# Cache pages fetched by GpSimd gathers instead of SyncE transfers, in a hybrid decoder step

## The reference

```python
def step(carry, phys):                      # one page of every sample
    c_blk = cache_ckv[layer, phys]          # (8, 128, 256)
    kp_blk = cache_kpe[layer, phys]         # (8, 128, 32)
    kn_blk, v_blk = _decompress(c_blk, w_ukv, g_kn)   # keys with RMS norm, values
    return _merge(carry, _attn_partial(qn, qp, kn_blk, kp_blk, v_blk, None)), None

carry, _ = lax.scan(step, init, page_table.T)
```

## Time and profile before

| | us |
|---|---|
| median of 3 runs | 1328.28 |
| the runs | 1329.59, 1326.9, 1328.28 |
| span of the profiled execution | 1324.8 |
| total time of the profiled execution | not listed apart from the span |
| TensorE busy in it | 1272.1 |
| VectorE, ScalarE, GpSimd busy | 716.4, 455.3, 152.3 |

### The profile page before, as it was taken

One profiled execution on the slowest core, in us unless ns is written; L12 is line 12 of the kernel. 1 busy time (PEld: TensorE's weight loads), 2 busy tenths in 40 slices (PEclk: granted clock), 3 DMA queues, 4 the chain that ended last, 5 costly groups with the idle time before them and its releaser, 6 DMA issues. The chain is left out here.

```text
span 1324.8 us, 25998 instructions
## 1 busy us (share of the span) xinstructions
PE 1272.1 (96%) x9479; PEld 741.2 (56%) x9479; DVE 716.4 (54%) x1781; ACT 455.3 (34%) x1108; POOL 152.3 (11%) x182
## 2 busy tenths in 40 slices
PE   6999999889999999999999988999999999989898
PEld 4545677656666666665545545666545455445343
DVE  4001448654666666564768776778666666530331
ACT  3001354233343434342445333443444444310220
POOL 0000326400010102033302320000000000000000
PEclk9999999999999999998999989999999999998999
DMA  6421121111111111310331113311343212101001
GB/s 214 161 81 52 34 64 33 52 40 38 37 34 43 38 34 39 72 42 20 95 98 46 41 37 122 126 53 37 101 120 107 84 55 66 39 0 36 16 16 36
DMA packets 82994, 81.48 MB, mean 62 GB/s; under 512 B 18946, under 2 KB 76611, under 8 KB 82868
## 3 DMA queue, kind: packets, MB, share of 16 engines
q1 hardware_dynamic: 80452, 73.87, 18.7%
q10 hardware_dynamic: 2416, 5.96, 1.3%
HBM read 75.72 MB, written 4.07 MB: 60 GB/s over the span
## 5 line engine op out<-in xcount | busy, mean ns | idle before, releaser
L499 PE MATMUL PS<-wk,c_T 128*128 128x512 f32 x1024 | 495.1, 607 | 0.0
L624 DVE TENSOR_REDUCE ssq<-sq__69 128x8 f32<-128x512 f32 x256 | 175.1, 684 | 182.4 <-ACT sq__69 L553 181.2
L499 PEld LDWEIGHTS PS<-wk,c_T 128*128 128x128 f32 x1024 | 176.9, 193 | 152.0 <-issue 139.5
L553 ACT ACTIVATE sq__69<-PS 128x512 f32<-128x512 f32 x256 | 152.6, 596 | 315.3 <-PE PS L499 314.3
L1482 PE MATMUL PS<-xnT,w_ring 128*128 128x276 f32 x416 | 102.6, 404 | 0.0
L1320 PE MATMUL PS<-w_ring,xnT 128*128 128x424 f32 x256 | 95.3, 529 | 0.9 <-DVE xnT L976 0.9
L1482 PEld LDWEIGHTS PS<-xnT,w_ring 128*128 128x128 f32 x416 | 78.9, 193 | 21.1 <-issue 4.1
L455 PE MATMUL PS<-cst,c_ring 128*128 128x128 f32 x512 | 80.0, 279 | 6.4 <-DVE dots_s L619 5.0
L455 PEld LDWEIGHTS PS<-cst,c_ring 128*128 128x128 f32 x512 | 60.6, 144 | 45.0 <-issue 40.5
L1320 PEld LDWEIGHTS PS<-w_ring,xnT 128*128 128x128 f32 x256 | 48.5, 193 | 45.0 <-issue 45.0
L2690 PE MATMUL PS<-w_g,nT 128*128 128x512 f32 x128 | 56.1, 595 | 0.0
(11 more groups left out here) (533 smaller groups left out, 1854.8 us busy)
## 6 DMA issues: line engine op xcount, KB each, us to landing
c_ring<-in_cache_ckv SPq DMA_DIRECT2D x256, 128.0 KB, 2.8
w_ring<-in_w_in SPq DMA_DIRECT2D x4, 1696.0 KB, 12.3
w_ring<-in_w_in SPq DMA_DIRECT2D x9, 512.0 KB, 5.1
r_ring<-in_cache_kpe SPq DMA_DIRECT2D x256, 16.0 KB, 1.7
w_o<-in_w_out SPq DMA_DIRECT2D x8, 512.0 KB, 4.5
w_g<-in_w_ple_gate SPq DMA_DIRECT2D x8, 512.0 KB, 3.6
xn<-in_x_prompt SPq DMA_DIRECT2D x4, 512.0 KB, 10.8
w_ring<-in_w_in SPq DMA_DIRECT2D x2, 1024.0 KB, 5.5
```

What stands on the lines that cost most here:

```text
L499: mm = pe.matmul(PS[:, NORM[v % 2], :], c_T[:, u % 2, k, t * P:(t + 1) * P], wk[:, k], start=(k == 0), stop=(k == 1))
L553: nc.scalar.activation(sq_[:, v % 2, :], PS[:, NORM[v % 2], :], ACT.Square).then_inc(no_sb, 1)
L624: dve.tensor_reduce(ssq[:, u % 2, t * H:(t + 1) * H], sq_[:, v % 2, :].rearrange("p (h c) -> p h c", h=H), AX.X, ALU.add).then_inc(red_sb, 1)
```

## The change

GpSimd requests all pages, as indirect transfers: each takes a column of row numbers, one a partition. VectorE builds two tables of them once (`gather_rows`, near the end of the preparation) from the page table, which is now loaded to all partitions: `token_rows` = page x 128 + partition, and `group_rows` = page x 32 + lane. Four gathers of 128 rows of 1 KB bring a step's latents, so a tile is now one page; one gather of 128 rows of 512 B brings its rotary keys. SyncE issues no pages; where its weight loads were placed by `on_sp.go`, they wait for semaphores of the other work. With the new layout each 32x32 block of the rotary tile can be turned by itself: VectorE does that in one instruction from `r_ring` to r_T, and TensorE's transpose and ScalarE's copy are gone. The `go` calls of GpSimd stand between its own work.

```diff
-        def latent_pages(u, page):
+        def at_step(u):
+            b, j = divmod(u, STEPS)
+            return j * BS + b
+
+        def latent_pages(u):
+            rows_of = io["cache_ckv"].rearrange("n p c -> (n p) c")
             for x in range(GT):
-                p4 = slice(32 * x, 32 * x + 32)
-                nc.sync.dma_start(c_ring[p4, u % RING, :, 0:KVL], ...)
+                at = at_step(u) * GT + x
+                nc.gpsimd.indirect_dma_start(c_ring[:, u % RING, x, 0:KVL], None, rows_of,
+                                             bass.IndirectOffsetOnAxis(ap=token_rows[:, at:at + 1], axis=0)
+                                             ).then_inc(c_in[u % RING], 16)
+
+        def pages_pool():
+            pool = nc.gpsimd
+            rows_of = io["cache_kpe"].rearrange("n (p t) c -> (n p) (t c)", t=GT)
             for u in range(NSTEP):
                 if u >= RING:
+                    pool.wait_ge(vv_ps, u - RING + 1)
+                    pool.sem_inc(slot_taken, 1)
                 if u >= ahead_pages:
+                    latent_pages(u)
                 if u >= R_RING:
-                    sp.wait_ge(tn_ps, u - R_RING + 1)
+                    pool.wait_ge(tn_sb, u - R_RING + 1)
+                nc.gpsimd.indirect_dma_start(r_ring[:, u % R_RING, :], None, rows_of,
+                                             bass.IndirectOffsetOnAxis(ap=group_rows[:, at_step(u):at_step(u) + 1], axis=0)
+                                             ).then_inc(r_in[u % R_RING], 16)
                 yield
...
-            def turn_r(u):                      # TensorE
-                pe.wait_ge(r_in[u % R_RING], 16 * GT * (u // R_RING + 1))
-                pe.wait_ge(k1_sb, u + 1)
-                pe.transpose(PS[:, TURN, 0:P], r_ring[:, u % R_RING, :], ident).then_inc(tn_ps, 1)
...
-            def turned_r(u):                    # ScalarE
-                act.wait_ge(tn_ps, u + 1)
-                nc.scalar.copy(r_T[:], PS[:, TURN, 0:P]).then_inc(tn_sb, 1)
...
+            def turned_r(u):                    # VectorE, at t == 0 ahead of scales(u - 1)
+                dve.wait_ge(r_in[u % R_RING], 16 * (u // R_RING + 1))
+                if u >= 1:
+                    dve.wait_ge(rp_ps, u)
+                dve.transpose(r_T[:].rearrange("c (p s) -> c s p", s=GT),
+                              r_ring[:, u % R_RING, :].rearrange("p (s c) -> p s c", s=GT)).then_inc(tn_sb, 1)
...
+                def gather_rows():              # VectorE, at p == 11 of the preparation
+                    dve.wait_ge(pages_in, 16)
+                    for x in range(GT):
+                        p4 = slice(32 * x, 32 * x + 32)
+                        ins = dve.tensor_scalar(group_rows[p4, :], pages[p4, x::GT], 32.0, con("lane")[p4, :], ALU.mult, ALU.add)
+                    ins.then_inc(group_idx, 1)
+                    dve.wait_ge(group_idx, 1)
+                    dve.tensor_scalar(token_rows[:], pages[:], float(P), con("token"), ALU.mult, ALU.add).then_inc(token_idx, 1)
...
+                    if p == 11:                 # GpSimd, behind diff(11)
+                        pool.wait_ge(token_idx, 1)
+                        pool.wait_ge(rw_ps, sum(c <= len(chunks) - 2 for c in chunk_of))
+                        for u in range(ahead_pages):
+                            latent_pages(u)
+                on_pool.go(PREP_SLOTS)          # behind p == 12
...
             for i in range(NP):                 # chunk_pool
+                on_pool.go(3)
                 pool.wait_ge(lc_sb, i + 1)
                 (three low products)
+                on_pool.go(7)
                 if i >= 1:
                     gated(i - 1)
+                on_pool.go(7)
...
+            on_pool.go(6)                       # seqs_pool
             for j in range(PAIRS):
                 if j == 1:
+                    on_pool.go(4)
                     gated(NT - 2)
                 (wait for gh_ps, six spread products)
+                on_pool.go(2)
+            on_pool.go(2)
             gated(NT - 1)
+            on_pool.go(4)
...
+            on_pool.go(2)                       # lat_pool; go(7) before each wait for h_ref, the rest at its end
...
-                    on_sp.go(2)                 # SyncE, w_o loads; w_g and wukv3 likewise on acc_sb
+                    sp.wait_ge(sc_ps, 2 * k + 1)
```

More of the change, by code:

```diff
@@ L18 @@
 I32 = mybir.dt.int32
+U32 = mybir.dt.uint32
 ALU = mybir.AluOpType
@@ L100, in shape_constants @@
     parts += [("headones", (s // HN == t // HN))]
-    parts += [("ones", np.ones((P, P)))]
+    parts += [("token", s), ("lane", s % 32)]
     parts += [("mod32", (s % 32 == t % 32))]
@@ L220, in build @@
         cols = place("cols", [P, NCOLS])
+        group_rows = place("group_rows", [P, NSTEP], U32)
         nat = place("nat", [P, NT, NAT])
@@ L241, in build @@
         nmax = place("nmax", [P, BS])
-        pages = place("pages", [1, BS * NPG], I32)
+        pages_at_ = place.at
+        pages = place("pages", [P, BS * NPG], I32)
+        token_rows = Region(nc, pages_at_, place.at)("token_rows", [P, BS * NPG], U32)
         sq_at_ = place.at
@@ L412, in build @@
         at_v, at_t = slice(0, KVL + 1), slice(0, P)
-        def page_numbers(u):
+        def at_step(u):
             b, j = divmod(u, STEPS)
-            return [nc.sync.value_load(pages[0:1, (j * BS + b) * GT + x:(j * BS + b) * GT + x + 1], min_val=0,
-                                       max_val=io["cache_ckv"].shape[0] - 1) for x in range(GT)]
-        def latent_pages(u, page):
+            return j * BS + b
+        def latent_pages(u):
+            rows_of = io["cache_ckv"].rearrange("n p c -> (n p) c")
@@ L508, in pages_pe @@
                 ahead = u + 1 < NSTEP
[L509 to L512, removed]
+                if t == 0 and u >= 2:
+                    turn_weights(u - 2)
                 if t == 1:
@@ L665, in pages_dve @@
                 ahead = u + 1 < NSTEP
-                if t == 0 and u >= 1:
-                    scales(u - 1)
+                if t == 0:
+                    turned_r(u)
+                    if u >= 1:
+                        scales(u - 1)
                 if t == 1:
@@ L687, in build @@
         whole_slots = len(slots) + 1
-        on_sp = Stream(pages_sp(), lambda slot: 2 if slot <= PREP_SLOTS else min(NSTEP, max(RING, (slot - 2) // GT + RING - 1)))
+        on_pool = Stream(pages_pool(), lambda slot: 2 if slot <= PREP_SLOTS else min(NSTEP, max(RING, (slot - 2) // GT + RING - 1)))
         on_pe, on_act, on_dve = (Stream(f(), lambda slot: slot) for f in (pages_pe, pages_act, pages_dve))
@@ L745, in _ @@
                         sp.wait_ge(xT_ps, NT + 1)
-                        sp.dma_start(pages[:], io["page_table"]).then_inc(pages_in, 16)
+                        sp.dma_start(pages[:], io["page_table"].to_broadcast([P, BS * NPG])).then_inc(pages_in, 16)
                         sp.wait_ge(c_norm, 1)
@@ L750, in _ @@
                         store(sp, io["kpe_sample"], s_rows[:, C_KPE:C_GA])
[L751 to L756, removed]
                 sp.wait_ge(stored, stores[0])
@@ L1173, in _ @@
                         ends(3)
+                        gather_rows()
                     if p == 12:
@@ L2432, in lat_pool @@
                 pool.sem_inc(kh_done, 1)
+            on_pool.go(LAT_SLOTS - 2 - 7 * NP)
         with nc.Block() as block:
@@ L2437, in _ @@
             def _(sp):
-                chunk_sp(sp)
                 seqs_sp(sp)
@@ L2527, in build @@
             "tg_ps gate_sb ps_ps ys_a ys_b").split())
+        TAIL_U = NSTEP - TAIL_SLOTS // GT
         units = [(h, i) for h in range(H) for i in range(NT - 1)]
@@ L2558, in _ @@
                 for k in range(KD):
-                    on_sp.go(GT)
+                    sp.wait_ge(acc_sb, TAIL_U + k)
                     sp.dma_start(w_g[:, k, :], io["w_ple_gate"][k * P:(k + 1) * P, :]).then_inc(w_g_in, 16)
                 for k in range(KVL // P):
-                    on_sp.go(GT)
+                    sp.wait_ge(acc_sb, TAIL_U + KD + k)
                     sp.dma_start(wukv3[:, k, :], io["w_ukv"][k * P:(k + 1) * P, :]).then_inc(wv_in, 16)
-                on_sp.go(TAIL_SLOTS - GT * (KD + KVL // P))
                 sp.wait_ge(rp_ps, NSTEP)
@@ L2585, in _ @@
                 sp.wait_ge(stored, stores[0])
+            @block.gpsimd
+            def _(pool):
+                on_pool.go(ATTN_SLOTS)
+                on_pool.go(TAIL_SLOTS)
             @block.tensor
```

22 lines of the change are left out of this document (3 added, 19 removed).

## The result

The changed kernel took 1437.11 us (median of 4 runs, 1434.87 to 1442.29) against 1327.59 of the kernel before: ratio 1.0832, 95% interval 1.0807 to 1.0857. Forecast were 1333.7 us and a range of 1324 to 1344. Later the same kernel, unaltered, ran on chip 15 of the same type: 1354.41 us against 1328.09, ratio 1.0193, interval 1.017 to 1.0216. That difference of 83 us for one program is the main finding; the experiments lead up to it.

A forecast was written before the change was run, and what follows sets the result against it. TensorE bounds the kernel, busy 1272.1 of 1324.8 us. Start 10.5, clock 1 and `spread` 2.5 less the gain of 8.6 give +5.4; with 3.5 from span to median, 1333.7 us, range 1324 to 1344.

The forecast's parts named there:

- Where does 5g = 6 us a step show?: GpSimd's queue: five gathers a step take 6 us; start costs 10.5 plus clock 1, `spread` 2.5, other places 0.
- (e): Stage ends: GpSimd's queue must be empty at each barrier; between 0 and 6 us, taken as 0.
- (a): Start: twelve gathers in GpSimd's queue delay `dots(0)`, loss 10.5 us, plus 1 us of lower clock.
- (c): Page 23's gathers stand between `spread(1)` and `spread(2)`, for which TensorE waits: loss 2.5 us, bounds 0.05 and 5.9.
- g: Queue time of one gather on GpSimd: 1.2 us, ends 0.71 and 1.87.
- gain of the layout and the transposes: TensorE's `turn_r` transposes and ScalarE's copies go, less VectorE's added work: 8.6 us gained.
- (b): Chunk stage: page 12's gathers stand ahead of `low` but fit in 8.0 us; loss 0, 2.6 at the upper end.
- T: Duration of VectorE's transpose of the rotary keys: 0.29 us, ends 0.13 and 0.69.
- A: Gathers on GpSimd are cheap, g under 0.90: faster, 1325 us at 0.71; chance 0.26.
- D: Start is covered, `dots(0)` not waiting for GpSimd's queue: only (c) stays, 1322 us; chance 0.02.
- B: GpSimd prepares gathers only while VectorE is idle and becomes the bound: tail 137 us longer, 1470 us; chance 0.05.
- C: VectorE's transpose is dear, T = 0.69: `dots` starts later, 9 us on top, 1342.5 us; chance 0.10.

The follow-up runs named there:

- i1: The changed kernel, unaltered, timed again on chip 15 beside the kernel before: 1354.41 us, ratio 1.0193.
- e1: Changed kernel's page layout and VectorE's turning of rotary keys, but every page copied by SyncE, no gathers; chip 7: 1319.42 us, ratio 0.9936 to the kernel before.
- e3: Changed kernel, but rotary pages copied by SyncE; the 256 latent gathers stay on GpSimd; chip 7: 1346.35 us.
- e4: As e1, all pages by SyncE, plus 320 GpSimd gathers of 16 bytes a partition into a buffer nobody reads; chip 7: 1342.86 us.
- h1: Changed kernel with two small GpSimd multiplications a step between the second and third latent gather; chip 5: 1357.69 us.
- h2: Changed kernel with two small GpSimd multiplications a step between the four latent gathers and the rotary one; chip 5: 1358.47 us.
- h6: Changed kernel with two small GpSimd multiplications a step ahead of the five gathers, which stay together; chip 5: 1356.51 us.
- g4: Changed kernel with small GpSimd work behind each latent gather not requested ahead, spacing the gathers; chip 0: 1382.39 us.
- e5: As e4, but two small GpSimd multiplications in each gather's place and no transfer by GpSimd; chip 0: 1327.85 us.
- f3: As e3, plus 64 small gathers of 16 bytes a partition into a spare buffer at the rotary gathers' place; chip 0: 1426.30 us.
- f2: Changed kernel with all 320 gathers, SyncE only reading page numbers and waiting for slots each step, copying nothing; chip 0: 1433.16 us.
- f1: Changed kernel with all 320 gathers, SyncE also copying four 512-byte pieces a step into a buffer nobody reads; chip 0: 1441.51 us.

## Why the prediction was wrong, point by point

**The step that failed** is "Where does 5g = 6 us a step show?": it prices a gather by its time in GpSimd's queue and nothing else. In it, place (e), the stage ends, is sized at 0 and measured 12.7 us, and the half clock behind the waits of (a) and (c) is sized at 1 us and measured about 6. Together these put even i1 above the range. The other 83 us of the first runs are in no term and no rival. The direction (slower) and g were right; the time was outside the range both times. The sizes below are read on quiet chips, as differences of i1 to e1 in the starts of the `norms` matmuls.

| term | forecast | measured |
|---|---|---|
| gain of the layout and the transposes | 8.6 | 8.1 (e1, medians) or 7.3 (traces) |
| (a) start, with the clock | 11.5 | 15.4 |
| (b) chunk stage, step 11 | 0 | 2.3 (0 to 0.8 in e3, e4, h1, h2, h6) |
| (c) `spread`, step 23 | 2.5 | 6.2 |
| (d) tail | 0 | 0.3 |
| (e) stage ends, steps 30 to 33 | 0 | 12.7 |
| the slow passages (chip or load) | not thought of | 0 or 83 |

The five terms of the gathers measure 36.9 us together; the spans of the two traces differ by 38.5 (i1's is of its slowest run) and the medians by 35.0. Forecast were 14.

**The gain.** T was 0.40, not 0.29, and e1's 8.1 us against 8.6 bear out the sum. It had one loss that wasn't forecast: TensorE waits 1.67 us for r_T at step 11, in e1 as in i1. The tail step went from 9.76 to 9.62 us, forecast 9.5 to 9.6. In i1 (as the earlier trace rows; one copy to the next):

```profile
993.92 0.68 DVE L604 COPY c_T<-PS 128x512 f32<-128x512 f32 x1
...
996.01 0.40 DVE L610 STREAM_TRANSPOSE r_T<-r_ring 128x128 f32<-128x128 f32 x1
...
1003.54 0.68 DVE L604 COPY c_T<-PS 128x512 f32<-128x512 f32 x1
```

**(a) and (c): the waits were right, the clock behind them was not.** In the first runs' trace `dots(0)` loaded at 270.7 us, forecast 271. That it fits so well is partly luck: the twelve gathers took 1.0 us more than 12 x 1.2, GpSimd's own work behind them 1.5 less. The first rotary page landed 1.5 us behind the end of its gather. (By the Trainium skill, DMA: Bandwidth & Descriptors, Latency and other measured facts, the forecast would be 271.4; the trace is with the row of SyncE's landing, 1.7 us.) TensorE waited 4.2 us for `spread`, forecast 3.7. But the long idle stretches are followed by matmuls at half clock, 1.2 GHz: in i1 the granted clock is 0.50 over 270 to 274 us and 0.56 over 274 to 278, and over 258 to 285 it is 0.70 against 0.94 in the kernel before. At `spread` in i1:

```profile
652.42 1.08 PE L467 MATMUL PS<-c_T,qp 128*32 128x128 f32 x16
653.27 1.08 PE L486 MATMUL PS<-c_ring,ew 128*32 128x257 f32 x8
654.29 3.01 PE L497 MATMUL PS<-wk,c_T 128*128 128x512 f32 x4
...
658.91 1.88 PE L497 MATMUL PS<-wk,c_T 128*128 128x512 f32 x4
```

The same four matmuls take 3.01 us behind the wait and 1.88 us one slot later. The 3.0 us more of waiting became 6.2. The 15.4 at the start are 1.4 of waiting for the very first gathered pages, which the forecast hadn't seen, 10.9 for r_T, 2.7 at half clock behind that, where I had charged 1, and 0.4 in later steps:

```profile
254.88 0.63 PE L458 MATMUL PS<-cst,c_ring 128*128 128x128 f32 x4 [1.42 <-DMA c_ring<-in_cache_ckv,token_rows]
...
271.91 0.80 PE L463 MATMUL PS<-r_T,q_rope 128*128 128x128 f32 x2 [10.91 <-DVE r_T L610]
```

A wait doesn't always bring the half clock. At step 11 the wait for r_T is 1.67 us in i1 and in e1, but the next four `norms` take 3.68 us in i1, while e1's clock stays at 1.00; against the kernel before the step costs 4.1 us in i1 and 1.8 in e1. The gathers add no waiting there, and why i1's clock fell isn't shown.

**(b)** held, but with nothing to spare. In i1 TensorE's weight loads wait for `low` twice, 0.8 us at most, and its matmuls not at all; with one more pause a step (h1, h2, h6) the matmuls wait 0.5, 0.7 and 0.2 us, in g4 2.5.

**(e) failed.** TensorE waits for the gathered pages at steps 30 to 33, and the barrier behind them is 3.2 us later. i1's waits:

```profile
PE PS L463 <- DVE r_T L610: 18.1, 5, 10.9
...
PE PS L458 <- DMA c_ring<-in_cache_ckv,token_rows: 7.6, 4, 4.7
PE PS L2606 <- PEq L209: 6.3, 1, 6.3
PE PS L2027 <- POOL spread L2119: 4.2, 1, 4.2
```

The row of L2606 (idle up to a barrier) stands at 3.1 us in e1. In e4, where nobody reads the gathers, steps 30 to 33 cost 3.7 of the 12.7 us, so 9 go with pages that come late; e3, with only the latent pages gathered, has 10.5 there. I had sized the last gathers of a stage and not those behind the stage's own work. GpSimd waits there for VectorE ahead of k_hat, 26.9 us in three times, with gathers behind it in the queue. The first time in i1:

```profile
751.02 1.04 POOL L2433 TENSOR_TENSOR k_hatp<-kn_all,hsp 128x512 f32<-128x512 f32 x1 [11.65 <-DVEq L2352]
...
761.04 1.01 POOL L427 DMA_INDIRECT c_ring<-in_cache_ckv,token_rows  x1 [0.83 <-POOL k_hatp L2429]
...
767.66 1.11 PE L458 MATMUL PS<-cst,c_ring 128*128 128x128 f32 x4 [4.69 <-DMA c_ring<-in_cache_ckv,token_rows]
```

The order of the queue is plain there: wait, k_hat, then the four gathers, then TensorE. That the wait ahead of k_hat is what makes the pages late wasn't tried apart.

**The rivals.** A falls with g = 1.25, D with the start, which waited for the queue. B falls: the mean of a gather is 0.95 us in the tail as elsewhere. The rule of the Trainium skill (SBUF — State Buffer, Who interferes with whom) on VectorE's two-port modes shows nowhere either, the pitch stays at 1.25 us; with one copy of 153 ns from SBUF to SBUF a step, this kernel is no hard trial of it. C was near in T (0.40) and wrong in effect. None of them held what cost most.

**The other 81 us** (spans 1437.2 and 1356.1) are TensorE busy 35 us longer and idle 46 us longer, 30.4 of them on "issue". The lower clock can be at most 27 of the 35, an estimate from the mean granted clocks, 0.954 over 1437.2 us and 0.971 over 1356.1. What is shown: the passages came with gathers (e5 has none, on chip 0, and takes 1327.85 us) and on chip 0 only, and nearly vanish when gathers stand 1.85 us apart (g4). In the first trace TensorE has 54 such gaps, and each has a gather starting within the 2.5 us before it or in it; such stretches are 39% of the time from 250 to 765 us. Not only TensorE is slow in them. In f3:

```profile
291.79 0.38 PE L1701 MATMUL PS<-AR,kT 64*64 64x128 f32 x2 [0.40 <-issue]
...
291.81 0.42 DVE L645 COPY dots_s<-PS 128x256 f32<-128x256 f32 x1 [3.17 <-remote]
...
293.22 0.35 PE L1701 MATMUL PS<-AR,kT 64*64 64x128 f32 x2 [1.06 <-issue]
...
293.35 0.60 ACT L573 ACTIVATE sq__72<-PS 128x512 f32<-128x512 f32 x1 [4.85 <-remote]
```

VectorE's copy starts at 291.81 although the matmuls that it waits for had ended before 290, and two of SyncE's register instructions, which take 3 to 147 ns just before, took 604 and 699 ns there (the one of 604 carries a wait, for a semaphore last raised at 280.28). So the sequencers of these four engines, or what passes semaphores between them, were held up together. GpSimd was not: its gathers keep their 1.25 us inside the passages. The instructions' own transfer doesn't explain it: 75 packets and 1.23 MB in both traces, and only 4 of the 54 gaps overlap such a packet. (The Trainium skill, Runtime: NRT & Kernel Launch, Instruction fetch mechanics, has a sequencer fetch its code in 16 KiB blocks over a DMA queue of its own; 75 packets of 16,384 bytes agree.) Why this happened on chip 0 and on none of the other three stays open, as does whether small gathers do it there: e4 was never run on that chip. (The updates don't tell: the fifth gather of a step has about 15 of 16 recorded on chip 0 whether it is full, as in f2, or small, as in f3.)

One rival isn't touched by any run: that the recording of the trace is what holds the sequencers up. The missing updates are missing records, since every wait for all sixteen was met, and in f1 they are missing for SyncE's tiny copies too (6.2 of 16). The passages stand where instructions, and so records, are densest. Every time on record is of an execution that was recorded. So it isn't shown that the 83 us would be there without the recording; in the tail of the first trace, though, the updates are missing (3.3 a latent gather) and there is no passage.

## What to carry to other kernels

Take the layout and leave the gathers: a page a tile with the rotary keys turned by VectorE and plain copies by SyncE is 0.6% faster than before, while the 320 gathers cost 35 us in quiet runs and 118 in the first ones. A queue that is in order must be priced at every place where its own work meets the new work, the ends of stages too. Where TensorE otherwise runs without a gap, a wait can cost more than its length, for the half clock behind it: here 1.2 times at the start (10.9 us of waiting, 13.6 lost), 2 times at `spread` (3.0 and 6.2), and once nothing more (e1's step 11). And before two experiments are compared, see that they ran on the same chip, or run the same kernel on both. Twelve runs here were planned without that.

## What the hardware showed that I had not expected

- A GpSimd gather of 128 rows costs 0.95 us and a pitch of 1.25 us whether a row has 1024, 512 or 16 bytes (e4).
- VectorE's transpose of 128x128 fp32 as 32x32 blocks takes 0.40 us, against 0.29 for a reduce of the same size.
- One kernel, two sets of runs: 1354.4 and 1437.1 us, while the kernel without gathers differs by 0.3% over four chips (1325.6 to 1329.3).
- On chip 0, while gathers run beside dense short matmuls, instructions of TensorE, VectorE, ScalarE and SyncE start late for some 2 us at a time, with gaps of 0.2 to 1.9 us on TensorE, and GpSimd keeps its pitch; only about 4 of a latent gather's 16 semaphore updates are recorded there.
